# Odd-layer attention by heads: transposed scores, masked bias tables made in the projection, output projection and router as a stage of their own

## The chip, the cores and the metric

The kernel runs on one NeuronCore of a Trainium2 chip, as one launch. The metric is the device time of one execution in microseconds (us). Times below are for the whole program of two layers; the change touches one part of the second layer. The engines are TensorE (PE in the profile, with its weight loads as PEld), VectorE (DVE), ScalarE (ACT), GpSimd (POOL) and SyncE (SP); DMAs are issued by SP, ACT and POOL.

## The reference, cut to what matters

Two layers over 1024 latent tokens (a grid of 16 rows of 64 columns) and 256 context tokens, model width 1024, float32. The second (odd) layer projects to q, k and v of 8 heads of width 64 and to a convolution branch. q and k are normalised per head. Each latent query sees 8 grid rows by 16 grid columns around it, with a bias per head and relative position, and all 256 context tokens:

```python
def row_block(args):
    qr, ridx, ri = args
    kr = jnp.take(kg, ridx, axis=1)[:, :, col_idx]
    vr = jnp.take(vg, ridx, axis=1)[:, :, col_idx]
    bias = jnp.transpose(rpb_cols[:, ridx - ri + NA_MAX_ROWS - 1], (0, 2, 1, 3))
    s_loc = jnp.einsum('bchd,bicjhd->bhcij', qr, kr, ...) * scale + bias
    s_ctx = jnp.einsum('bchd,bshd->bhcs', qr, k_ctx, ...) * scale
    p = jax.nn.softmax(jnp.concatenate([s_loc..., s_ctx], axis=-1), axis=-1)
    ...
```

The heads' outputs and the convolution's (512 columns each) go through the output projection (1024 x 1024), a gate and the residual; then come a second norm and a router with 16 logits, and the mixture of experts. In the odd layer only latent tokens are needed behind the attention.

## The kernel before, in words

Tokens lie in tiles of 128: 8 latent (LT) and 2 context (CT) ones. Stages follow each other with a barrier of all engines between them; in a stage every engine has its own program and waits on semaphores. Matrix products whose exactness matters are split: an operand is rounded to a high part (`hi`, type fp32r) and a rest (`lo`), and three products hi*hi, hi*lo, lo*hi are summed in PSUM.

`project_odd` (tiles `po_...`, L941) loops over 10 token tiles. `NormStage` loads, normalises, transposes and modulates a tile: ACT rounds it (L339), POOL makes the rest (`rest_lo`, L343) and the inverse root (`root`, L305), DVE scales the next tile (L310). PE makes q, k and v (72 matmuls of 512 columns). For the per-head norms ACT squares, DVE sums (L1057), POOL raises to -1/2 (L1029), DVE multiplies (L1067, L1068). PE transposes k (L1086), ACT and DVE split it into `kT1_hi` and `kT1_lo` (L1007, L1074), which stay in SBUF with `v1`. q goes to DRAM (`q_d`). SP writes each row of the bias table 64 times to DRAM (`rpb_d`, L981), so that a read with a skewed stride gives a table over query and key columns.

`attend(nc, k, 1, ...)` (tiles `at_...`, L1199) walks over `AttendPlan.events`, an order written out for all engines: for each of 8 query tiles 8 heads. One (tile, head) is a unit: PE makes scores with the 128 queries on partitions (three products, L1597) over 4 or 5 key tiles and 2 context tiles, DVE adds the table and takes the maximum (L1474, L1478, L1482), ACT takes the exponential with the row sum (L1356), PE transposes the probabilities tile by tile (L1610), ACT and DVE copy them (L1369, L1493), and PE multiplies each 128 x 128 piece with 64 columns of v (L1575). Tables come by DMA for each head and each of three groups of tiles (`load_table`, L1336), and POOL adds the masks (L1409, L1413). Between the units of a tile lie the steps of the tile before: `heads`, `mixed`, two halves of the output projection (L1563), the residual on POOL (L1435), the norm, and the router (also L1563, 24 matmuls of 16 columns).

`attend_even` (L1730) is layer 0's attention. It is not changed, and its lines L1858, L1981, L2070, L2071 and L2078 work on transposed scores: keys on partitions, 512 columns of queries.

## Time and profile before

| | |
|---|---|
| median of 3 runs | 3467.13 us (3462.18 to 3471.53) |
| the profiled execution, its own time | 3476.95 us |
| its span | 3475.2 us |
| projection of the odd layer, 2052.4 to 2306.4 us | 254.0 us |
| attention, output projection, router of the odd layer, 2306.4 to 2904.6 us | 598.2 us |
| busy over the span: PE, DVE, ACT, POOL | 79%, 44%, 29%, 15% |

The stages' borders are the first DMA that SP issues in each. Busy shares are averages over stages with different limits. [...]

### The profile page before, as it was taken

The numbers are of one execution on the slowest core, as the hardware profiler recorded it, in microseconds if no ns is written. First come the engines' busy times: TensorE is split into PE (matmuls) and PEld (weight loads), VectorE is DVE, ScalarE is ACT, GpSimd is POOL, SyncE is SP. The second block draws the span as 40 slices with busy tenths as digits, with TensorE's granted clock in tenths as the row PEclk, the third lists the DMA queues.
The fourth block names the chain that finished last, engine by engine and source line by source line (L and its number), as shares of the span: only waits on it lengthen the run. The fifth ranks groups of instructions, "written<-read, shape, count | busy, mean of one in ns | idle before, by whom it ended". The sixth has DMA issues, their size and how long they took to land. (4 is left out here: it accounts for less than half of the span.)

```text
span 3475.2 us, 34184 instructions
## 1 busy us (share of the span) xinstructions
PE 2733.7 (79%) x11887; PEld 2073.8 (60%) x11888; DVE 1535.6 (44%) x2403; ACT 1012.6 (29%) x1342; POOL 531.5 (15%) x485
## 2 busy tenths in 40 slices
PE   5499788897844999997068957868899992899991
PEld 0488455565611888885055325757788882688781
DVE  2255543334222566464623723333333332566754
ACT  1122232332302455452111112222222220455640
POOL 0233112011120000000230002320300112100001
PEclk9999798897956999998588978975666675899995
DMA  9110353110167777663700022242111113658855
GB/s 376 54 42 34 104 181 141 32 55 28 43 204 288 257 261 261 249 223 122 266 25 6 12 57 71 68 97 69 39 43 40 40 40 138 243 215 329 307 218 211
DMA packets 244213, 476.78 MB, mean 137 GB/s; under 512 B 85773, under 2 KB 99067, under 8 KB 237948
## 3 DMA queue, kind: packets, MB, share of 16 engines
q1 hardware_dynamic: 172312, 354.27, 29.4%
q0 software_dynamic: 19632, 65.66, 5.2%
q10 hardware_dynamic: 52148, 55.28, 4.8%
q8 instruction: 72, 1.18, 0.1%
q14 instruction: 49, 0.40, 0.0%
HBM read 387.70 MB, written 87.45 MB: 137 GB/s over the span
## 5 line engine op out<-in xcount | busy, mean ns | idle before, releaser
L2505 DVE TENSOR_TENSOR ex_gu_lo<-mw_gu,ex_gu_hi 128x2048 fp32r<-128x2048 f32 x128 | 287.4, 2288 | 78.0 <-ACT ex_gu_hi L2425 77.7
L2425 ACT ACTIVATE ex_gu_hi<-mw_gu 128x2048 fp32r<-128x2048 f32 x128 | 237.5, 1910 | 166.4 <-DVE ex_y L2552 160.6
L2078 PE MATMUL at_ps_o<-at_pT,at_v_one 128*128 128x512 f32 x336 | 186.3, 638 | 1.7 <-ACT at_pT L1858 1.7
L2583 PE MATMUL ex_ps_g<-ex_gu_hi,ex_xT_hi 128*128 128x512 f32 x408 | 169.7, 416 | 8.4 <-issue 5.2
L2583 PE MATMUL ex_ps_y<-ex_d_hi,ex_hT_hi 128*128 128x512 f32 x408 | 166.7, 409 | 9.1 <-DVE ex_d_lo L2505 7.7
L1858 ACT ACTIVATE at_pT<-at_ps_s 128x512 f32<-128x512 f32 x168 | 99.5, 595 | 233.5 <-PE at_ps_s L2071 233.2
L2505 DVE TENSOR_TENSOR ex_d_lo<-mw_d,ex_d_hi 128x2048 fp32r<-128x2048 f32 x64 | 143.8, 2289 | 53.4 <-ACT ex_d_hi L2425 53.4
L2583 PE MATMUL ex_ps_g<-ex_gu_lo,ex_xT_hi 128*128 128x512 f32 x408 | 164.4, 403 | 0.0
L2583 PE MATMUL ex_ps_g<-ex_gu_hi,ex_xT_lo 128*128 128x512 f32 x408 | 164.2, 402 | 0.0
L2583 PE MATMUL ex_ps_y<-ex_d_lo,ex_hT_hi 128*128 128x512 f32 x408 | 161.9, 397 | 0.0
L2583 PE MATMUL ex_ps_y<-ex_d_hi,ex_hT_lo 128*128 128x512 f32 x408 | 161.9, 397 | 0.0
L2583 PE MATMUL ex_ps_u<-ex_gu_hi,ex_xT_hi 128*128 128x512 f32 x408 | 161.2, 395 | 0.0
L2583 PE MATMUL ex_ps_u<-ex_gu_lo,ex_xT_hi 128*128 128x512 f32 x408 | 161.2, 395 | 0.0
L2583 PE MATMUL ex_ps_u<-ex_gu_hi,ex_xT_lo 128*128 128x512 f32 x408 | 161.1, 395 | 0.0
L1356 ACT ACTIVATE at_s<-at_s,at_nmx 128x768 f32<-128x768 f32 (+1 forms) x64 | 63.3, 989 | 318.4 <-DVE at_nmx L1482 318.4
L1575 PEld LDWEIGHTS at_ps_o<-v,at_pT 128*128 128x128 f32 x832 | 154.5, 283 | 1.4 <-issue 1.4
L2051 PE MATMUL at_ps_t<-k_both,at_q_both 128*128 128x512 f32 (+1 forms) x208 | 112.5, 581 | 54.5 <-DVE at_mx L1968 37.9
L1575 PE MATMUL at_ps_o<-v,at_pT 128*128 128x64 f32 x832 | 154.9, 363 | 0.5 <-ACT at_pT L1369 0.2
L2400 POOL TENSOR_TENSOR ex_at<-ex_slots,ex_nil 128x1 int32<-128x1 int32 x53 | 16.6, 312 | 804.1 <-PE ex_ps_x L2577 799.1
L1968 DVE TENSOR_REDUCE at_mx<-at_ps_t 128x1 f32<-128x512 f32 (+1 forms) x208 | 115.9, 583 | 48.0 <-PE at_ps_t L2051 46.6
L320 PE MATMUL pc_pt<-ident,pc_x 128*128 128x128 f32 x64 | 14.9, 409 | 148.2 <-DVE pc_x L310 148.2
L2425 ACT ACTIVATE ex_d_hi<-mw_d 128x2048 fp32r<-128x2048 f32 x64 | 119.1, 1909 | 28.3 <-DVE ex_y L2527 19.7
(456 smaller groups left out, 6400.2 us busy)
## 6 DMA issues: line engine op xcount, KB each, us to landing
mw_gu<-in_moe_w_gate SPq DMA_DIRECT2D x32, 2048.0 KB, 10.4
mw_gu<-in_moe_w_up SPq DMA_DIRECT2D x32, 2048.0 KB, 15.4
mw_d<-in_moe_w_down SPq DMA_DIRECT2D x32, 2048.0 KB
y_d<-ex_y ACTq DMA_DIRECT2D x51, 512.0 KB
mod_mod_w<-in_ada_w SPq DMA_DIRECT2D x24, 1024.0 KB, 11.0
ro_mod_w<-in_ada_w SPq DMA_DIRECT2D x24, 1024.0 KB, 19.8
y_d<-at_zero POOLq DMA_DIRECT2D x36, 512.0 KB, 5.2
x_d<-at_x SPq DMA_DIRECT2D x18, 512.0 KB, 2.6
```

The costliest lines, as they stand in the source:

```text
L320: mm = self.nc.tensor.transpose(self.pt[h][:, q, :], self.x[i % 2][:, c * P:(c + 1) * P], self.k.ident[:, :])
L1356: nc.scalar.activation(s[u % 3][:, 0:n], s[u % 3][:, 0:n], ACT.Exp, bias=nmx[:, u % 3:u % 3 + 1], accum_out=sums[:, i % 2, h:h + 1]).then_ ...
L1575: mm = nc.tensor.matmul(ps_o[i % 2][:, h * HD:(h + 1) * HD], pT[u % 2][:, c, :], values(kt, h), start=(c == 0), stop=(c == len(kts) - 1), ...
L1858: nc.scalar.activation(pT[u % 3][:, :], ps_s[u % 3][:, :], ACT.Exp).then_inc(S["exp_done"], 1)
L1968: nc.vector.tensor_reduce(mx[:, hd, c:c + 1], ps[:, :, :].rearrange("p c t -> p (c t)")[:, 0:runs[c][1]], AX.X, ALU.max).then_inc(read, 1)
L2051: nc.tensor.matmul(ps[:, :, :].rearrange("p c t -> p (c t)")[:, 0:n], q_both[i % 2][g][:, j * P:(j + 1) * P], k.k0_both[:, g, a:a + n], st ...
L2078: nc.tensor.matmul(ps_o[g][:, :], v_one[:, kt, g:g + 2, :].rearrange("p a d -> p (a d)"), pT[u % 3][:, :], start=(u == plan.first[i, g]), ...
L2400: nc.gpsimd.tensor_tensor(at[:, :], slots[:, bass.ds(within(n, most), 1)], nil[:, :], ALU.add).then_inc(S["at_ready"], 1)
L2425: nc.scalar.activation(dst, src, ACT.Copy).then_inc(sem, 1)
L2505: sub = lambda dst, a, b, sem: nc.vector.tensor_tensor(dst, a, as_f32(b), ALU.subtract).then_inc(sem, 1)
L2583: mm = nc.tensor.matmul(out, a[:, c, :], b[:, c, cols], start=(c == 0 and j == 0), stop=(c == chunks - 1 and j == 2))
```

## The change

The projection no longer keeps k and v in SBUF. It also transposes q, splits it, and POOL stores q, k (high and rest, transposed) and v to DRAM by its own DMA queue. POOL also makes the bias tables with the column mask in them: in 16 parts it loads a part of a mask table (`skews`, 480 KB broadcast), adds the bias rows, and stores 480 KB to `rows_d`. There are two tables, for queries and for keys on partitions.

The attention works on units (head, half of the queries): 16 units of 8 steps, each step one key tile against up to 512 queries. First come maxima: for each query tile one product with rounded operands, whose maximum over keys becomes a shift; it is transposed and put as a 65th row into the query operand. Then per step: two products for the scores, DVE adds the table, ACT takes the exponential, one product with v beside a block of ones gives outputs and sums. All operands of a head come by 19 DMAs; two heads' buffers exist. The output projection and the router run as a new stage behind it, over 8 tiles.

```diff
-def project_odd(nc, k, w_in, q_norm, k_norm, rpb):
+def project_odd(nc, k, w_in, q_norm, k_norm, rpbs, skews):
...
+        PART = 8
...
+                        nc.scalar.activation(v[j % 2][:, :], ps_v[:, :], ACT.Copy).then_inc(S["v_copied"], 1)
                         act.wait_ge(S["kT_full"], i)
+                        nc.scalar.activation(k_hi[j % 2][:, :, :], ps_kT[:, :].rearrange("p (c t) -> p c t", c=4), ACT.Copy
+                                             ).then_inc(S["kT_hi"], 1)
                         if j < LT:
-                            act.wait_ge(S["q_ready"], i)
-                            act.dma_start(k.q_d[j * P:(j + 1) * P, :], qk[:, 0:BW]).then_inc(S["q_out"], 16)
+                            act.wait_ge(S["qT_full"], i)
+                            nc.scalar.activation(q_hi[j % 2][:, :, :], ps_qT[:, :].rearrange("p (c t) -> p c t", c=4), ACT.Copy,
+                                                 scale=HD ** -0.5).then_inc(S["qT_hi"], 1)
...
+                def store_heads(j):
+                    p, t = j % 2, slice(j * P, (j + 1) * P)
+                    pool.wait_ge(S["kT_done"], j + 1)
+                    parts = [(k.kh_d, k_hi), (k.kl_d, k_lo)]
+                    if j < LT:
+                        pool.wait_ge(S["qT_done"], j + 1)
+                        parts += [(k.qh_d, q_hi), (k.ql_d, q_lo)]
+                    for dst, src in parts:
+                        pool.dma_start(dst[:, t].rearrange("(c p) t -> p c t", p=P), as_f32(src[p][:, :, :])).then_inc(head_out[p], 16)
+                    pool.wait_ge(S["v_copied"], j + 1)
+                    pool.dma_start(k.v_d[t, :], v[p][:, :]).then_inc(head_out[p], 16)
+                def load_skew(n):
+                    o, part = divmod(n, GRID_W // PART)
+                    pool.dma_start(skew[n % 2][:, :, :].rearrange("p c x -> p (c x)"),
+                                   skews[o, part * PART * P:(part + 1) * PART * P].partition_broadcast(8 * 15)).then_inc(S["skew_in"], 16)
+                def mask_rows(n):
+                    o, part = divmod(n, GRID_W // PART)
+                    pool.wait_ge(S["rows_in"], 32)
+                    pool.wait_ge(S["skew_in"], 16 * (n + 1))
+                    if n >= 2:
+                        pool.wait_ge(S["rows_out"], 16 * (n - 1))
+                    nc.gpsimd.tensor_tensor(rows[n % 2][:, :, :], skew[n % 2][:, :, :], bc(bias_rows[o][:, :], 1, PART), ALU.add
+                                            ).then_inc(S["rows_made"], 1)
+                    pool.wait_ge(S["rows_made"], n + 1)
+                    pool.dma_start(k.rows_d[o].rearrange("h r c x -> (h r) c x")[:, part * PART:(part + 1) * PART, :], rows[n % 2][:, :, :]
+                                   ).then_inc(S["rows_out"], 16)
+                    if n + 1 < 2 * GRID_W // PART:
+                        load_skew(n + 1)
...
+                        if j:
+                            store_heads(j - 1)
+                            for n in (2 * j - 2, 2 * j - 1):
+                                if n < 2 * GRID_W // PART:
+                                    mask_rows(n)
+                store_heads(NT - 1)
...
+                        if j < LT:
+                            dve.wait_ge(S["qT_hi"], i)
+                            nc.vector.scalar_tensor_tensor(q_lo[j % 2][:, :, :], ps_qT[:, :].rearrange("p (c t) -> p c t", c=4), HD ** -0.5,
+                                                           as_f32(q_hi[j % 2][:, :, :]), ALU.mult, ALU.subtract).then_inc(S["qT_done"], 1)
...
+                    if j < LT:
+                        pe.wait_ge(S["q_ready"], j + 1)
+                        if j:
+                            pe.wait_ge(S["qT_done"], j)
+                        for c in range(4):
+                            mm = nc.tensor.transpose(ps_qT[:, c * P:(c + 1) * P], qk[:, c * P:(c + 1) * P], k.ident[:, :])
+                        mm.then_inc(S["qT_full"], 1)
...
-def key_plan(l, tile):
...
-class AttendPlan:
...
-def attend(nc, k, l, w_out, colmask, rowmask):
...
+class OddPlan:
+    def __init__(self):
+        self.units = [(h, g) for h in range(8) for g in range(2)]
+        self.steps, self.first, self.last = [], {}, {}
+        for u, (h, g) in enumerate(self.units):
+            self.first[u] = len(self.steps)
+            local = self.local(g)
+            self.steps += [(u, LT, 0, 4)] + local[:3] + [(u, LT + 1, 0, 4)] + local[3:]
+            self.steps[self.first[u]:] = [(u, *s[1:]) for s in self.steps[self.first[u]:]]
+            self.last[u] = len(self.steps) - 1
...
+        nu = len(self.units)
+        for u in range(nu):
+            for s in range(self.first[u], self.last[u] + 1):
+                at = s - self.first[u]
+                if u + 1 < nu and at < 4:
+                    self.event('max', u + 1, at)
+                if at == 2 and u and self.units[u - 1][0] % 2:
+                    self.event('normal', u - 1)
+                if u + 1 < nu and at == 6:
+                    self.event('shift', u + 1)
+                if s % 4 == 3 and s // 4 < 16:
+                    self.event('weights', s // 4)
+                if s + 2 < len(self.steps):
+                    self.event('scores', s + 2)
+                self.event('values', s)
+            self.event('drain', u)
+        self.event('normal', nu - 1)
+    def local(self, g):
+        return [(0, kt, max(kt - 2, 0) if kt > 3 else 0, min(kt + 3, 4)) if g == 0 else
+                (0, kt, 0 if kt < 7 else 1, min(kt - 1, 2) if kt < 4 else 4) for kt in range(2 * g, 2 * g + 6)]
...
+def attend_odd(nc, k, w):
...
+                def rows(dst, o, h, r0, n):
+                    ap = bass.AP(k.rows_d.tensor, ((o * 8 + h) * 15 + r0) * GRID_W * P + P // 2 - 1,
+                                 [[P - 1, GRID_W], [GRID_W * P, n], [1, GRID_W]])
+                    sp.dma_start(dst.rearrange("p (s c) -> p s c", s=n), ap).then_inc(head_in[h % 2], 16)
+                for h in range(8):
+                    p = h % 2
+                    if h >= 2:
+                        sp.wait_ge(S["valued"], plan.last[2 * (h - 2) + 1] + 1)
+                    r = slice(h * HD, (h + 1) * HD)
+                    for dst, src in ((qb[p][0:HD, :], k.qh_d), (qb[p][HD:P, :], k.qh_d), (kb[p][0:HD, :], k.kh_d), (kb[p][HD:P, :], k.kl_d)):
+                        sp.dma_start(as_f32(dst), src[r, :]).then_inc(head_in[p], 16)
+                    for half in range(2):
+                        s = slice(half * GRID_W, (half + 1) * GRID_W)
+                        rows(inner[p][s, half * GRID_W:(half + 8) * GRID_W], 0, h, 3, 8)
+                        for g, r0 in enumerate((5, 1)):
+                            rows(edge[p][s, g, :], 0, h, r0 - half, 10)
+                    sp.dma_start(as_f32(qr[p][0:HD, :]), k.ql_d[r, :]).then_inc(head_in[p], 16)
+                    sp.dma_start(as_f32(k1[p][0:HD, :]), k.kh_d[r, :]).then_inc(head_in[p], 16)
+                    for half in range(2):
+                        s = slice(half * GRID_W, (half + 1) * GRID_W)
+                        rows(innerT[p][s, (half + 1) * GRID_W:(half + 9) * GRID_W], 1, h, 4, 8)
+                        for g, r0 in enumerate((1, 5)):
+                            rows(edgeT[p][s, g, :], 1, h, r0 - half, 10)
...
+                    if what == 'scores':
+                        s, (u, kt, c0, c1) = i, steps[i]
+                        n = (c1 - c0) * P
+                        if s >= 3:
+                            act.wait_ge(S["valued"], s - 2)
+                        if kt < LT:
+                            act.wait_ge(S["added"], plan.added[s])
+                            src = sb[(plan.added[s] - 1) % 2]
+                        else:
+                            act.wait_ge(S["scored"], s + 1)
+                            src = ps_s[s % 2]
+                        nc.scalar.activation(pT[s % 3][:, 0:n], src[:, 0:n], ACT.Exp).then_inc(S["exp_done"], 1)
...
+                        if (j < 2) == (g == 0):
+                            slot = (2, 0)[j % 2] * GRID_W
+                            nc.vector.tensor_tensor_reduce(junk[j % 2][:, 0:512], ps[:, 0:512], edge[p][:, g, slot:slot + 512], 1.0, -3.0e38, ALU.add,
+                                                           ALU.max, mx[g][:, j, 0:1])
+                            nc.vector.tensor_reduce(mx[g][:, j, 1:2], ps[:, 512:512 + CT * P], AX.X, ALU.max).then_inc(read, 1)
+                        else:
+                            nc.vector.tensor_tensor_reduce(junk[j % 2][:, :], ps[:, 0:10 * GRID_W + CT * P], inner[p][:, :], 1.0, -3.0e38, ALU.add,
+                                                           ALU.max, mx[g][:, j, 0:1]).then_inc(read, 1)
...
+                        dve.wait_ge(S["scored"], s + 1)
+                        nc.vector.tensor_tensor(sb[(m - 1) % 2][:, 0:n], ps_s[s % 2][:, 0:n], tab[:, slot * GRID_W:slot * GRID_W + n], ALU.add
+                                                ).then_inc(S["added"], 1)
+                    elif what == 'normal':
+                        h, g = units[i]
+                        dve.wait_ge(S["drained"], i + 1)
+                        nc.vector.reciprocal(sums[:, g, :], sums[:, g, :]).then_inc(S["inverted"], 1)
...
+                        if s == plan.first[u]:
+                            emptied(pe, 'shift', u)
+                        if s >= 2:
+                            if steps[s - 2][1] < LT:
+                                pe.wait_ge(S["added"], plan.added[s - 2])
+                            else:
+                                pe.wait_ge(S["exp_done"], s - 1)
+                        keys, q = slice(kt * P, (kt + 1) * P), slice(g * 512 + c0 * P, g * 512 + c1 * P)
+                        nc.tensor.matmul(ps_s[s % 2][:, 0:n], kb[p][:, keys], qb[p][:, q], start=True, stop=False)
+                        nc.tensor.matmul(ps_s[s % 2][:, 0:n], k1[p][0:HD + 1, keys], qr[p][0:HD + 1, q], start=False, stop=True
+                                         ).then_inc(S["scored"], 1)
+                    elif what == 'values':
+                        s, (u, kt, c0, c1) = i, steps[i]
+                        h, g = units[u]
+                        n = (c1 - c0) * P
+                        pe.wait_ge(S["exp_done"], s + 1)
+                        if s == plan.first[u] and u >= 2:
+                            pe.wait_ge(S["drained"], u - 1)
+                        nc.tensor.matmul(ps_o[g][:, c0 * P:c1 * P], vo[h % 2][:, kt, :, :].rearrange("p a d -> p (a d)"), pT[s % 3][:, 0:n],
+                                         start=(s == plan.first[u]), stop=(s == plan.last[u])).then_inc(S["valued"], 1)
...
+def output_odd(nc, k, w):
...
+                for i in tiles:
...
+                        mm.then_inc(S["g_full"], 1)
+                        if i and not half:
+                            route(i - 1)
+                    if i:
+                        scores(i - 1)
+                route(LT - 1)
+                scores(LT - 1)
...
```

## Rows read from the trace of the kernel before

**Rows 1.** Windows: projection, attention to router, one query tile, layer 0's attention

```profile
core 0: us, PE busy (x) PEld busy (x) DVE busy (x) ACT busy (x) POOL busy (x), PEclk, DMA share, GB/s
2052.40:2306.40 254.00, 191.99 (x792) 151.00 (x792) 87.77 (x176) 55.72 (x84) 70.12 (x39) 0.88 0.26 70
2306.40:2904.60 598.20, 517.21 (x2528) 463.00 (x2528) 193.18 (x626) 140.25 (x266) 90.06 (x64) 0.66 0.19 53
2599.00:2667.00 68.00, 65.13 (x328) 58.83 (x328) 23.30 (x76) 16.63 (x32) 5.24 (x4) 0.70 0.11 37
380.00:1000.00 620.00, 512.40 (x1884) 341.58 (x1884) 241.72 (x406) 191.25 (x330) 88.96 (x92) 0.86 0.27 90
```

**Rows 2.** Groups by line and shape, same query tile, 2599 to 2667

```profile
L1575 PE MATMUL at_ps_o<-v,at_pT 128*128 128x64 f32 x112 | 20.6, 360 | 0.0
...
L1610 PE MATMUL at_ps_t<-ident,at_s 128*128 128x128 f32 x56 | 13.3, 373 | 0.0
...
L1563 PE MATMUL at_ps_g<-at_w_hi,at_aT_hi 128*128 128x512 f32 x16 | 7.2, 449 | 0.0
```

**Rows 3.** GpSimd's timeline, one tile of the projection

```profile
2186.10 2.91 POOL L1029 TENSOR_TENSOR po_r<-po_stat,mhalf 128x16 f32<-128x16 f32 x1 [2.20 <-DVE po_stat L1059]
2190.41 1.79 POOL L1033 TENSOR_TENSOR po_qk<-po_qk,po_gains 128x512 f32<-128x512 f32 x1 [1.40 <-DVE po_qk L1068]
2203.19 2.40 POOL L343 TENSOR_TENSOR po_lo<-po_hf,po_hi 128x1024 fp32r<-128x1024 f32 x1 [10.99 <-ACT po_hi L339]
...
2208.30 2.91 POOL L1029 TENSOR_TENSOR po_r<-po_stat,mhalf 128x16 f32<-128x16 f32 x1 [2.20 <-DVE po_stat L1059]
```

**Rows 4.** Timeline of all engines, the same tile

```profile
2197.50 0.60 PE L1086 MATMUL po_ps_kT<-ident,po_qk 128*128 128x128 f32 x4
...
2198.77 0.69 DVE L1074 TENSOR_TENSOR kT_lo<-po_ps_kT,kT_hi 128x512 fp32r<-128x512 f32 x1 [7.71 <-ACT kT_hi L1007]
...
2199.38 2.64 DVE L331 TENSOR_SCALAR po_hf<-po_pt,po_cols 128x128 f32<-128x128 f32 x8
```

**Rows 5.** DMAs issued by GpSimd: duration of the issue, time to landing

```profile
L1910 POOL DMA_DIRECT2D y_d<-at_zero x36: 533/533/672, 381.8 to 553.8; - x36
...
DMA to landing us min/median/max: 3.0/5.2/13.1
```

**Rows 6.** Timeline of layer 0, full clock, a float32 product and the next instruction

```profile
647.58 1.02 PE L2078 MATMUL at_ps_o<-at_pT,at_v_one 128*128 128x512 f32 x2
...
648.04 0.80 PE L2031 MATMUL at_ps_g<-at_w_hi,at_aT_hi 128*128 128x512 f32 x1
```

**Rows 7.** Timeline, half clock, two products of 512 columns in a row

```profile
1785.08 0.63 PE L352 MATMUL pc_ps_g<-cw_w_lo,pc_hi 128*128 128x512 f32 x1
...
1785.51 0.63 PE L352 MATMUL pc_ps_g<-cw_w_hi,pc_lo 128*128 128x512 f32 x1
```

**Rows 8.** VectorE's groups by shape, attention of the odd layer

```profile
L1474 DVE CUSTOM_DVE_ANT_0 at_s<-at_ps_s,at_table 128x320 f32<-128x320 f32 x64 | 29.6, 489 | 31.0 <-POOL at_table L1413 15.5 <-PE at_ps_s L1597 13.2 <-issue 1.1
L1478 DVE TENSOR_SCALAR_CACHE_REDUCE at_s<-at_ps_s 128x256 f32<-128x256 f32 x64 | 27.0, 422 | 3.8 <-PE at_ps_s L1597 2.5
...
L1529 DVE TENSOR_TENSOR at_tmp<-at_ps_g,at_gate 128x512 f32<-128x512 f32 x16 | 11.1, 692 | 115.8 <-PE at_ps_g L1563 115.8
```

**Rows 9.** VectorE's reciprocal in layer 0's attention

```profile
L1981 DVE RECIPROCAL at_sums<-at_sums 128x512 f32<-128x512 f32 x10 | 33.4, 3337 | 9.3 <-ACT at_total L1868 9.3
```

**Rows 10.** ScalarE's exponential in layer 0's attention

```profile
L1858 ACT ACTIVATE at_pT<-at_ps_s x168: 577/597/612, 409.5 to 938.7; 128x512 f32<-128x512 f32 x168
```

**Rows 11.** DMA queues, 2324 to 2330: only 256-byte packets of tables

```profile
q10 hardware_dynamic: 4701, 1.17, 129.9%
```

**Rows 12.** DMA issues, 2242 to 2272: KB, us to landing

```profile
rpb_d<-po_bias_rows SPq DMA_DIRECT2D x1, 3840.0 KB, 27.7
```

**Rows 13.** Window 2312 to 2315, start of the attention: last number GB/s

```profile
2312.00:2315.00 3.00, 0.00 (x0) 0.00 (x0) 0.00 (x0) 0.00 (x0) 0.00 (x0) 0.50 1.04 363
```

**Rows 14.** Window of one router product, line L1563 alone

```profile
2604.79:2608.47 3.68, 3.68 (x24) 3.68 (x24) 0.72 0.41 131
```

944 lines of the change are left out of this document (407 added, 537 removed).

## Prediction, made before the changed kernel was run

> **What bounds the kernel now.** I read the windows by stage first. The change touches two stages of the span of 3475.2 us: the odd layer's projection, 254.0 us, and attention with output projection and router, 598.2 us [rows 1]. In the second PE is busy 517 of 598 us, and in a steady query tile 65.1 of 68.0 us; DVE has 23 and ACT 17 of those 68. So PE sets the end, at a mean clock of only 0.70 in that tile (layer 0's attention: 0.86) [rows 1]. The groups of that tile show where PE's time goes: 20.6 us for 112 products with only 64 columns, 13.3 us for 56 transposes of probabilities, while the output projection's 48 products of 512 columns take about 3 x 7 us [rows 2]. Head by head, PE spends its time on instructions that stream few columns.
>
> The projection is bound by a loop through several engines, not by PE: GpSimd's power (L1029) starts at 2186.10 and again at 2208.30, a period of 22.2 us [rows 3]. Between them GpSimd ends L1033 at 2192.20 and idles 11.0 us until `rest_lo` (L343). That waits for PE's transposes, DVE's modulation and ACT's rounding [rows 3, 4]; behind it on GpSimd stand `root` and the next power, and for these wait DVE's scaling and the next tile's products.
>
> **Projection.** It adds four transposes of q (0.4 us, by those of k) and DVE's q rest (0.69 us as L1074), both ahead of the modulation L331 [rows 4]: +1.1 us a tile if nothing else is later. ACT's copies (0.6 us) and the dropped q store move nothing.
>
> GpSimd's new work, put into the 11.0 us: five stores a tile. One issue takes 0.53 us with 128 pieces [rows 5]; four of the new ones have 512 pieces, which no row shows. I take 1.0 us for each (bounds 0.53 and four times that, 2.1), in all 4.6 us with v's 0.6. A mask add on 120 x 1024 elements costs 2.4 us as L343 [rows 3], with a store and a load issued behind it 3.6 us; two a tile. The second add waits for the mask part whose load was issued just before: landing took 3.0 to 13.1, median 5.2 us for 512 KB [rows 5]; I take 5.0. Sum: 4.6 + 3.6 + 5.0 + 3.6 = 17 us, 6 more than are free. Then GpSimd is the loop: 28 us for the eight tiles that make tables (8 x 6 = 48), 2 us for the rest, 4 us for the last stores: 254 + 54 = **308 us**. Bounds: stores at 0.53 and landing in 3.0 give 13 us of work: 254 + 8 x 2 + 6 = 276. Stores at 2.1 and landing at 6 give 22: 254 + 88 + 6 = 348. The dropped `rpb_d` write (27.7 us [rows 12]) ended before the stage did; worth 0.
>
> **Attention, PE and DVE of a unit.** The removed work is the whole 598. Of a new unit PE streams 3328 columns once for maxima, 3328 twice for scores and 3328 for values in float32. A float32 product of 512 columns takes 0.46 us at full clock, 647.58 to 648.04, two passes of 0.23 [rows 6]; at 1.2 GHz one pass takes 0.43 [rows 7]. That is 32.5 passes: 7.5 us, or 14.0 at 1.2 GHz. DVE has more: from 256 and 320 columns (0.42 and 0.49 us) a slope of 1.05 ns per column [rows 8]. A maximum over 896 columns is 1.09 + 0.08, one over 512 and 256 is 0.69 + 0.08 + 0.42: four together 4.7 us. Six adds on 2304 columns are 3.3 us, minus-maximum 0.2. In half of the units comes a reciprocal of 3.34 us [rows 9], 1.7 on average, in the middle of the maxima. All maxima lie in the first four steps: there DVE needs 8.5 us and gaps, 9.3, and PE waits. The last four steps have PE: 2.6 us, about 1.2 us while ACT puts the shift row in place ahead of the next unit's first scores, and the chain product, add, exponential (0.60 us [rows 10]): 4.5. Sum 13.8 us at full clock; at half clock the first part is PE's 10 and the second 7: 17. I take U = **15 us**. ACT's 7 us a unit are hidden.
>
> **Attention, loads of a head.** 12 of the 19 loads are tables in pieces of 256 bytes, with v 2.16 MB. Alone, such pieces moved at 1.17 MB in 6 us, 195 GB/s [rows 11]: 11.1 us. The other 1.77 MB and 0.5 MB of output weights go at some 300 GB/s, between that and the 363 of large pieces [rows 13]: 7.6 us; with 2.3 us to land L = **21 us** (bounds: 17, all near 300 to 363; 33, all at the 3.93 MB in 27.7 us of the table write [rows 12], with landing). A head's loads are released when the head two before it is done, but the maxima of its first unit stand in the second unit of the head before: they have one unit of cover, 15 us, not two. PE and DVE both wait at the head of their queues, everything behind them too. Head period: 21 + 15 = 36 us instead of 30.
>
> Stage: 2 + 20 us for head 0 (all covers gone), 8 for four maxima, the exponential's table and a shift, 30 for head 0's units: 60. Six periods of 36: 216. The last head 30. Last reciprocal and splits 9, barriers 5. **320 us**. Bounds: U 13, L 17: 18 + 7 + 26 + 6 x 30 + 26 + 12 = 269. U 17, L 33: 33 + 9 + 34 + 6 x 50 + 34 + 15 = 425.
>
> [...]
>
> **Output stage.** Per tile 48 products: 11.2 us at 0.233; the router's 24 took 3.7 [rows 14]; eight transposes 0.9. The norm's chain runs beside the next tile's first half: DVE's product 0.69, GpSimd's adds, DVE's and GpSimd's passes over 1024 columns about 8 us, about PE's 3 + 5.6. At half clock a tile is 27. I take 17.5, as the small products let the clock fall: 140, with 10 to fill (gate rows, first split) and 15 for the last norm and router: **165 us** (148 to 200).
>
> **Sum.** 308 + 320 + 165 = 793 against 852.2: 59 us less. The profiled execution took 3476.95 us and becomes 3418; it lies 9.8 us over the median, so the median of 3467.13 becomes **3408 us**.
>
> **Rivals.**
> (a) The head loads are hidden after all, L under U: for it speaks that alternate halves of the partitions are filled; 36 us less: 3372. 15%.
> (b) GpSimd's additions fit in its idle 11 us (loads land in 3 us, stores cost 0.5): 6 a tile less, 1.1 stays: 3367. 12%.
> (c) The clock stays at 1.2 GHz through the attention: rows show 0.70 and 0.66 in the stage of before and 0.50 in its start, where PE is often idle [rows 1, 13]. U = 17 lengthens 16 units and not the loads: 20 us with fewer recoveries, with 10 in the output stage 3438. 12%. [...]
> (d) Slower: the head loads crawl. At 142 GB/s as the table write [rows 12] L is 33 and each of six periods 12 longer: 3480. It decides from L = 31. Against it: loads of the same pieces ran at 195 GB/s [rows 11]. 9%.
> (e) GpSimd's stores at 3 us each or more, issue by issue: 8 us x 8 more, 3472. 5%.
> (f) Both (a) and (b): 3331. 5%.
> The forecast itself: 42%, with its own range of 3375 to 3440.
>
> **Numbers.** 0.3% is about 10 us, what a measurement of this kernel tells from no change. Slower: (d), part of (e) and of the forecast's upper tail: 12%. Same: 7%. Faster: 81%. The range takes in (a), (b), (c), and (e): 3330 to 3475.
>
> **What would show it.** Right: in the projection GpSimd's L1029 every 27 to 29 us and no idle time before `rest_lo`; in the attention PE and DVE waiting some 6 us, six times, for loads of a head, once in 36 us; DVE the fullest engine of a unit's first half, with reciprocals of 3.3 us. The forecast is wrong if GpSimd's period stays near 23 or goes beyond 34, if the head period is 30 or 48, or if the output stage's tiles take over 20 us.

## The result, and the profile after

The changed kernel takes 3489.05 us (median of 4 runs, 3487.29 to 3496.10) beside 3466.55 us for the kernel before (4 runs, 3462.18 to 3471.53): a ratio of 1.0058 with a 95% interval of 1.0041 to 1.0076. It is slower by 0.6%, where 1.7% faster was forecast, and it lies outside the range. The kernel before, run again beside later experiments, had medians of 3465 to 3473 us; beside the highest of these the slowdown would be 16 us and not 22. The profiled execution took 3487.29 us, with a span of 3485.5.

I read the stages first. The windows go from the first transfer of one stage on the SP queue to that of the next: projection, attention, output stage. PEclk is the TensorE clock that was granted, as a share of full speed; its mean over the span is 0.84 in the kernel before and 0.86 in this one.

```profile
core 0: us, PE busy (x) PEld busy (x) DVE busy (x) ACT busy (x) POOL busy (x), PEclk, DMA share, GB/s
2051.30:2380.80 329.50, 208.74 (x824) 164.00 (x824) 92.63 (x184) 59.19 (x92) 158.49 (x134) 0.80 0.43 120
2380.80:2743.20 362.40, 218.46 (x736) 139.28 (x736) 148.11 (x299) 109.42 (x201) 50.52 (x50) 0.77 0.62 99
2743.20:2915.00 171.80, 145.34 (x640) 121.35 (x640) 34.32 (x58) 23.12 (x41) 53.79 (x40) 0.81 0.28 99
```

Beside [rows 1]: the projection has grown from 254.0 to 329.5 us, and the 598.2 us of attention, output projection and router are now 362.4 + 171.8 = 534.2. That is 75.5 us lost and 64.0 won. What stands behind took 570.6 us and takes 570.5; of the 11.5 us the span shows 10.3, as the projection began 1.1 earlier. In the attention PE's busy time fell far, and is only 218 of 362 us, with DVE at 148: no engine is full there. The DMA share has risen from 0.19 to 0.62. The question is what everyone waits for.

**Projection.** GpSimd's timeline of one tile, to set beside [rows 3]; in brackets the idle time ahead and what ended it.

```profile
2142.64 2.91 POOL L1073 TENSOR_TENSOR po_r<-po_stat,mhalf 128x16 f32<-128x16 f32 x1 [2.21 <-DVE po_stat L1112]
2146.95 1.79 POOL L1077 TENSOR_TENSOR po_qk<-po_qk,po_gains 128x512 f32<-128x512 f32 x1 [1.40 <-DVE po_qk L1121]
2148.68 0.88 POOL L1033 DMA_DIRECT2D kh_d<-po_k_hi  x1
2149.57 0.76 POOL L1033 DMA_DIRECT2D kl_d<-po_k_lo  x1
...
2152.38 2.40 POOL L1049 TENSOR_TENSOR po_rows<-po_skew,po_bias_rows 120x1024 f32<-120x1024 f32 x1
...
2155.61 0.54 POOL L1039 DMA_DIRECT2D po_skew<-in_k_skew  x1
2163.96 2.40 POOL L1049 TENSOR_TENSOR po_rows<-po_skew,po_bias_rows 120x1024 f32<-120x1024 f32 x1 [7.81 <-DMA po_skew<-in_k_skew]
...
2167.73 2.35 POOL L343 TENSOR_TENSOR po_lo<-po_hf,po_hi 128x1024 fp32r<-128x1024 f32 x1
2170.03 0.56 POOL L305 TENSOR_TENSOR po_rstd<-po_ms,mhalf 128x1 f32<-128x1 f32 x1
2172.79 2.91 POOL L1073 TENSOR_TENSOR po_r<-po_stat,mhalf 128x16 f32<-128x16 f32 x1 [2.20 <-DVE po_stat L1112]
```

The power comes 30.15 us later, and ahead of L343 there is no idle time left where [rows 3] had 10.99. So GpSimd is the loop, as forecast. The one hole is the 7.81 us ahead of the second mask addition, which waits for the load that L1039 has just issued; it was forecast at 5.0. The five stores cost 3.7 us, not 4.6.

This isn't so in all eight tiles that make tables. In the first five the wait is 7.8 to 8.4 us and the period 30.1 to 30.7; in the last three the wait is 5.5 to 5.6, and the one full period among them is 27.95. The first line is SP's, the second GpSimd's in the sixth of these tiles:

```profile
2156.19 0.32 SPq L275 DMA_DIRECT2D po_x<-x_d  x1
...
2313.42 2.40 POOL L1049 TENSOR_TENSOR po_rows<-po_skew,po_bias_rows 120x1024 f32<-120x1024 f32 x1 [5.58 <-issue]
```

In each of the five tiles with the long wait SP issues the load of a later token tile (L275, 512 KB) 0.6 to 1.9 us after GpSimd has issued the mask part's; in the other three there is no such load left. The five stores stand ahead of the mask load in all eight. So in this trace the long wait goes with the second load beside it, and without it the landing was close to the 5.0 us forecast.

**Attention.** The queue's issues on SP show when a head's loads are released, and PE's timeline when its first maximum begins.

```profile
2443.95 1.11 SPq L1753 DMA_DIRECT2D at_qb<-qh_d  x2
...
2492.80 1.11 SPq L1753 DMA_DIRECT2D at_qb<-qh_d  x2
```

```profile
2471.05 0.80 PE L1924 MATMUL at_ps_t<-at_kb,at_qb 128*128 128x512 f32 x1 [15.03 <-DMA at_edgeT<-rows_d]
2522.50 0.79 PE L1924 MATMUL at_ps_t<-at_kb,at_qb 128*128 128x512 f32 x1 [11.09 <-DMA at_edgeT<-rows_d]
```

From the release at 2443.95 to the first maximum at 2471.05 are 27.1 us, for the next head 2492.80 to 2522.50, 29.7. These are the two longest of six: the others take 26.0, 23.9, 24.1 and 23.4, and the mean is 25.7. From the first maximum to the next release are 21.75 and, to 2536.91, 14.41 us, and so on in turn, with a mean of 18.7 over five. The releases of heads 2 and 7 stand at 2443.95 and 2668.05: a mean period of 44.8 us, forecast at 36. Windows in one such load, the last three with all engines still:

```profile
2446.00:2449.00 3.00, 3.00 (x12) 2.00 (x12) 2.84 (x7) 1.64 (x3) 0.00 (x0) 1.00 1.16 203
2449.00:2452.00 3.00, 2.89 (x12) 1.60 (x10) 2.16 (x6) 1.14 (x3) 1.82 (x2) 1.00 1.06 249
...
2461.00:2464.00 3.00, 0.00 (x0) 0.00 (x0) 0.00 (x0) 0.00 (x0) 0.00 (x0) 0.50 1.03 208
2464.00:2467.00 3.00, 0.00 (x0) 0.00 (x0) 0.00 (x0) 0.00 (x0) 0.00 (x0) 0.50 1.37 156
2467.00:2470.00 3.00, 0.00 (x0) 0.00 (x0) 0.00 (x0) 0.00 (x0) 0.00 (x0) 0.50 1.23 139
```

What moves in a window is told by its packets. In the first, more than half of the bytes are v's, in pieces of 256 bytes on ScalarE's queue; in the third more than a third are output weights. The second holds q, k and output weights in pieces of some 3 to 5 KB and next to nothing else: 249 GB/s, and two such windows in the next head's load show 186 and 171. The last two hold table pieces of 256 bytes alone: 156 and 139, and 159 in the next head. I had taken 300 and 195.

A second wait was not foreseen. This is the timeline of DVE, GpSimd, ScalarE and PE around a reciprocal:

```profile
2477.45 3.35 DVE L1901 RECIPROCAL at_sums<-at_sums 128x512 f32<-128x512 f32 x1
...
2480.89 1.26 POOL L1836 TENSOR_TENSOR at_a<-at_total,at_sums 128x512 f32<-128x512 f32 x1 [22.34 <-DVE at_sums L1901]
...
2482.18 0.63 ACT L1806 ACTIVATE ow_a_hi<-at_a 128x512 fp32r<-128x512 f32 x1 [4.95 <-POOL at_a L1836]
2482.84 0.60 ACT L1784 ACTIVATE at_pT<-at_ps_s 128x512 f32<-128x512 f32 x1
...
2483.49 0.79 PE L1949 MATMUL at_ps_s<-at_qb,at_kb 128*128 128x512 f32 x1 [4.41 <-ACT at_pT L1784]
```

ScalarE's rounding L1806 waits for GpSimd's product, that for DVE's reciprocal, and the exponentials are queued behind the rounding: PE idles 4.41 us. Over the stage PE waits so seven times, 29.5 us in all; three of the seven lie in a unit that covers a load. Behind the wait PE starts at a granted clock of 0.50 and keeps it up to 2489 (0.69 on the mean from 2483.49 to 2492.80).

**Output stage.** Windows in one tile:

```profile
2780.00:2782.00 2.00, 2.00 (x11) 2.00 (x11) 0.00 (x0) 0.00 (x0) 0.00 (x0) 0.50 0.20 76
2782.00:2784.00 2.00, 2.00 (x6) 1.71 (x7) 0.88 (x3) 0.00 (x0) 0.56 (x1) 0.50 0.00 0
2784.00:2786.00 2.00, 2.00 (x6) 1.52 (x6) 0.64 (x1) 0.00 (x0) 1.28 (x1) 0.50 0.00 0
...
2788.00:2790.00 2.00, 2.00 (x13) 1.64 (x12) 0.14 (x1) 0.00 (x0) 0.00 (x0) 1.00 0.96 295
```

In a tile PE waits 2.07 us for DVE ahead of the router's products of 16 columns; within these the granted clock falls to 0.50 and stays there through some nine of the wide products: they start 0.43 us apart, and 0.23 at 1.00. From tile to tile it takes 20.0 us in five cases of six, not 17.5.

### The profile page after: what moved, and what is told of

It reads as the page before. It is cut to its first block and busy times, and to the rows that moved or that the text cites. A ratio compares the mean times of both kernels' runs of the same rounds, so it can differ in the third digit from the quotient of the medians.

```text
span 3485.5 us, 31738 instructions
## 1 busy us (share of the span) xinstructions
PE 2594.6 (74%) x10767; PEld 1883.2 (54%) x10768; DVE 1530.2 (44%) x2142; ACT 1007.7 (29%) x1326; POOL 632.4 (18%) x606
## 5 line engine op out<-in xcount | busy, mean ns | idle before, releaser
L1959 PE MATMUL at_ps_o<-at_pT,at_vo 128*128 128x512 f32 (+3 forms) x256 | 129.8, 593 | 1.4 <-ACT at_pT L1784 1.4
L926 PE MATMUL pc_ps_c<-pc_yT,pc_diag 128*128 128x512 f32 x248 | 107.3, 593 | 1.6 <-ACT pc_acc L766 1.6
L1567 PEld LDWEIGHTS at_ps_t<-k_both,at_q_both 128*128 128x128 f32 x208 | 43.9, 211 | 118.3 <-DVE at_mx L1484 73.0
```

The lines of the kernel that those rows point to most:

```text
L926: mm = nc.tensor.matmul(ps_c[:, :], diag[c][:, t, :], yT[:, c, q * QT + t:q * QT + t + QT], start=(t == 0), stop=(t == CONV - 1))
L1567: nc.tensor.matmul(ps[:, :, :].rearrange("p c t -> p (c t)")[:, 0:n], q_both[i % 2][g][:, j * P:(j + 1) * P], k.k0_both[:, g, a:a + n], st ...
L1959: nc.tensor.matmul(ps_o[g][:, c0 * P:c1 * P], vo[h % 2][:, kt, :, :].rearrange("p a d -> p (a d)"), pT[s % 3][:, 0:n], start=(s == plan.fi ...
```

## The experiments

Ratios are against the kernel before; the changed kernel's is 1.0058. A saving in us against the changed kernel is the difference of the two ratios times 3467, good to some 8 us; where less matters, I go by the length of the stage in the profiled execution, measured as above.

### e1_ahead: the mask parts loaded two ahead

```diff
-                    if n + 1 < 2 * GRID_W // PART:
-                        load_skew(n + 1)
+                    if n + 2 < 2 * GRID_W // PART:
+                        load_skew(n + 2)
...
                 load_skew(0)
+                load_skew(1)
```

with one semaphore for each of the two buffers, for loads and for stores.

> Projection only: the load of mask part n+2 is issued after the add of part n, so every load has a tile's time to land; nothing is left out. Theory (the second add of a tile waits 7.8 to 8.4 us for a load issued right before it, and this wait is on the loop that sets the tile's period): GpSimd's power comes every 22.5 to 24 us instead of 30.1 to 30.7, the projection goes from 329.5 to about 277 us, and the kernel takes about 3437 us. Rival 1 (the 7.8 us are transfers queued behind the tile's own stores, so the load lands as late however early it is issued): period 28 to 30, 3475 us. Rival 2 (store issues and adds themselves fill the loop): period 26 to 27, 3460 us.

Measured: 3439.43 us, ratio 0.9912 (0.9886 to 0.9937), 51 us saved. The projection took 278.8 us. GpSimd's timeline:

```profile
2184.24 2.40 POOL L1051 TENSOR_TENSOR po_rows<-po_skew,po_bias_rows 120x1024 f32<-120x1024 f32 x1
...
2188.03 2.41 POOL L1051 TENSOR_TENSOR po_rows<-po_skew,po_bias_rows 120x1024 f32<-120x1024 f32 x1
...
2192.41 2.40 POOL L343 TENSOR_TENSOR po_lo<-po_hf,po_hi 128x1024 fp32r<-128x1024 f32 x1 [0.62 <-ACT po_hi L339]
```

No idle time is left between the additions, and GpSimd is 0.62 us early at L343: from the power at 2174.53 to the next at 2197.53 are 23.0 us. The wait for the mask part was on the loop with its full length; both rivals fall. The rest of GpSimd's new work, some 11 us a tile, fits almost exactly into what was idle before; the stage is still 25 us longer than it was, half of it from the last tile of latent tokens on.

### e2_mask_first: both mask parts ahead of the five stores

```diff
                         if j:
-                            store_heads(j - 1)
                             for n in (2 * j - 2, 2 * j - 1):
                                 if n < 2 * GRID_W // PART:
                                     mask_rows(n)
+                            store_heads(j - 1)
```

> Projection only, nothing left out: GpSimd makes both mask parts of a tile before it issues the tile's five stores. Theory (a mask part lands in 7.8 us and not in 5 because it is queued behind 1.3 MB of the tile's stores): the wait ahead of the second add falls to 4.5 to 5.5 us, the period from 30.4 to about 27.5, kernel 20 to 25 us below the changed kernel, about 3468 us. Rival (the 7.8 us are the load's own: 120 partitions filled from one row): the wait stays at 7 to 8.5, period 30 or more, kernel within 5 us of the changed one, about 3490 us.

Measured: 3483.32 us, ratio 1.0020 (1.0005 to 1.0034), 13 us saved; by the stage 6 us (323.1 us). The wait is 6.66 us in the first tile and 5.6 to 5.9 in the other seven, the periods are 29.0 and then 28.0 to 28.6. So the result lies between the two expectations, but it doesn't show that the stores were what the load waited for. The new order also moved the mask load away from the load of a token tile, which is now issued 4 us or more behind it (2.6 in the first tile); and in the changed kernel, where no token tile is loaded beside it, the wait is 5.5 us with all five stores ahead. Both runs fit a load of 5.5 to 6 us of its own and 2 to 3 more for the 512 KB beside it. No run moves that load alone.

### e3_no_tables: no tables for heads 2 to 7

```diff
-                    for half in range(2):
+                    for half in range(2 if h < 2 else 0):
                         s = slice(half * GRID_W, (half + 1) * GRID_W)
...
```

and the same for the transposed tables, with the counts of the waits to match.

> Leaves out the 12 table loads of heads 2 to 7 (these heads use the tables of heads 0 and 1). Theory (the load of a head, 27 to 30 us against a cover of one unit, sets the head period): a head's remaining 2.1 MB land in 8 to 12 us, inside a unit; PE has no wait for a load at a head's first maximum, the head period goes from 44 to 49 us to 32 to 36, attention from 362 to 295 us, kernel about 3420 us. Rival 1 (the units themselves have grown, by the wait behind the reciprocal and a clock of 1.2 GHz, and would fill the period anyway): period 40 or more, kernel 3460 us or more.

Measured: 3422.17 us, ratio 0.9859 (0.9834 to 0.9884), 69 us saved; attention 292.7 us, head period 32.4. At heads 2 to 7 PE waits for a load three times, 2.2, 1.6 and 0.3 us, where it waited six times and 61.9 us in all. The load of a head set the period. The stages behind the router take their old time here, so the kernel's times can be compared. The waits at the reciprocals stayed, 4.8 us the longest, and the period is at 32 in spite of them.

### e4_long_pieces and e9_whole: what makes the load long

In e4_long_pieces a table load becomes

```diff
-                    sp.dma_start(dst.rearrange("p (s c) -> p s c", s=n), ap)
+                    sp.dma_start(dst, k.kh_d[h * HD:(h + 1) * HD, 0:n * GRID_W])
```

> Loads other data (rows of the stored keys) of the same bytes, into the same half of the partitions, in pieces of 2048 and 2560 bytes instead of 256, in place of the tables. Theory (the pieces of 256 bytes make the load of a head long): load 15 to 19 us instead of 27 to 30, head period 36 to 38, kernel about 3435 us. Rival 1 (the bytes, or the 64 partitions that each transfer fills, are what takes the time): load 25 us or more, head period 43 or more, kernel 3475 us or more.

In e9_whole each pair of transfers into 64 partitions becomes one into 128:

```diff
-                    for dst, src in ((qb[p][0:HD, :], k.qh_d), (qb[p][HD:P, :], k.qh_d), (kb[p][0:HD, :], k.kh_d), (kb[p][HD:P, :], k.kl_d)):
-                        sp.dma_start(as_f32(dst), src[r, :]).then_inc(head_in[p], 16)
+                    for dst, src in ((qb[p][:, :], k.qh_d), (kb[p][:, :], k.kh_d)):
+                        sp.dma_start(as_f32(dst), src[0:P, :]).then_inc(head_in[p], 16)
...
+                    rows(inner[p][:, GRID_W:8 * GRID_W], 7)
+                    for g in range(2):
+                        rows(edge[p][:, g, :], 10)
```

> Loads other data in place of q, k and the tables, as in e4_long_pieces in pieces of 1792 to 5120 bytes, but each transfer into all 128 partitions (9 transfers on the SP queue instead of 18, each twice as large; per head 3% fewer bytes). Theory (a transfer that fills 64 partitions moves at 220 to 250 GB/s, and this is why long pieces saved only 4 us of the load): 300 to 360 GB/s, from a head's release to its first maximum 16 to 18 us instead of 22.8, head period 36 to 38, kernel about 3445 us. Rival (it is the bytes, at what this path reads and writes, whatever the partitions): 220 to 250 GB/s, 21 to 23 us, kernel within 8 us of e4_long_pieces, about 3480 us.

Both change the attention's values, and with them what the router chooses: behind the router these two take 584.7 and 584.3 us instead of 570.5. Their own times (e4_long_pieces 3480.94 us, ratio 1.0029, 1.0014 to 1.0044; e9_whole 3447.90 us, ratio 0.9939, 0.9917 to 0.9960) hold 14 us that don't belong to the question, so I read the attention: 339.9 and 298.6 us, against 362.4. First e4_long_pieces, the head released at 2443.18, PE's first maximum and two windows:

```profile
2465.95 0.79 PE L1922 MATMUL at_ps_t<-at_kb,at_qb 128*128 128x512 f32 x1 [10.68 <-DMA at_edgeT<-kh_d]
```

```profile
2458.00:2461.00 3.00, 0.00 (x0) 0.00 (x0) 0.00 (x0) 0.00 (x0) 0.00 (x0) 0.50 1.04 222
2461.00:2464.00 3.00, 0.00 (x0) 0.00 (x0) 0.00 (x0) 0.00 (x0) 0.00 (x0) 0.50 1.07 227
```

and e9_whole, the head released at 2443.97:

```profile
2461.79 0.79 PE L1918 MATMUL at_ps_t<-at_kb,at_qb 128*128 128x512 f32 x1 [5.74 <-DMA at_edgeT<-kh_d]
```

```profile
2446.00:2449.00 3.00, 3.00 (x13) 2.02 (x12) 2.87 (x7) 1.61 (x3) 0.00 (x0) 1.00 1.06 362
2449.00:2452.00 3.00, 2.92 (x12) 1.60 (x10) 2.16 (x6) 1.14 (x3) 1.82 (x2) 1.00 1.02 342
2452.00:2455.00 3.00, 2.13 (x8) 1.29 (x9) 0.29 (x1) 1.34 (x4) 0.00 (x0) 1.00 1.06 277
2455.00:2458.00 3.00, 1.05 (x7) 0.79 (x5) 0.29 (x1) 2.50 (x5) 1.25 (x1) 1.00 1.04 225
```

The load of head 2 goes from 27.1 to 22.8 us with long pieces (4.3 less, and 22 us of attention), and to 17.8 with whole transfers (5.0 less again, with 3% fewer bytes). In e4_long_pieces the full windows of the load show 222 to 258 GB/s and its mean is 209; the period is 41.3 us, above what the theory on pieces allowed. In e9_whole the mean over the load is 263, from 362 in its first full window down to 225, and the period is 35.5. So of the 9.3 us between the changed kernel's load and e9_whole's, pieces of 256 bytes are less than half; v keeps its short pieces in both. The larger part goes with transfers into 64 partitions. What in such a transfer is slow, e9_whole doesn't separate: it also has about half as many transfers, twice as large, and two of its ten on the SP queue, those of `qr` and `k1`, still fill 64 partitions (its expectation speaks of nine, all whole).

### e5_early_tables: the maxima's tables released a unit earlier

```diff
                     if h >= 2:
+                        sp.wait_ge(S["nmx_done"], 2 * (h - 2) + 2)
+                    for half in range(2):
...
+                        rows(inner[p][s, half * GRID_W:(half + 8) * GRID_W], 0, h, 3, 8, max_in)
+                        for g, r0 in enumerate((5, 1)):
+                            rows(edge[p][s, g, :], 0, h, r0 - half, 10, max_in)
+                    if h >= 2:
                         sp.wait_ge(S["valued"], plan.last[2 * (h - 2) + 1] + 1)
```

The maxima wait for `max_in` (these six and the four of q and k), the first scores of the head for `head_in` (the other nine).

> Nothing is left out: the six tables for the maxima of head h are loaded as soon as the last maxima of head h-2 are done, a unit earlier than before; q and k follow at the old release and have a semaphore with these tables, the other nine loads have one of their own and are waited for at the first scores, a unit later. Theory (what is late is the release, not the rate): the wait of 14 us at a head's first maximum falls to under 2, nothing takes its place, head period 32 to 36, kernel about 3420 us. Rival 1 (the rate: 4 MB a head at 150 to 180 GB/s take 25 us of the period however early they start, and the wait moves to the first scores): head period 38 to 42, kernel 3455 us.

Measured: 3403.98 us, ratio 0.9815 (0.9790 to 0.9840), 84 us saved; attention 278.4 us, head period 31.3. Of these 84 us 68 lie in the five periods, 9 ahead of head 2's release and 7 behind head 7's. In PE's timeline from 2438 to 2502, over two heads, the waits of 2 us and more are these:

```profile
2460.92 0.80 PE L1958 MATMUL at_ps_s<-at_qb,at_kb 128*128 128x512 f32 x1 [4.78 <-ACT at_pT L1790]
2481.18 0.58 PE L1958 MATMUL at_ps_s<-at_qb,at_kb 128*128 128x256 f32 x1 [4.15 <-ACT at_pT L1790]
```

The bytes and their pieces are all still there, and from head 2 on no load is waited for: with this order of releases and waits the slow transfers cost nothing. Rival 1 falls. Two things were changed at once, the earlier release of six tables and the later wait for nine of the other loads; which carries how much, no run separates. The 9 us ahead of head 2 belong to the second, as the loads of the first heads wait for no release: PE's wait at head 0 is 28.0 us instead of 38.5. That, and q and k released late (waits of 2.2 and 1.6 us), is most of what e3_no_tables saved less.

### e6_split_later and e12_late: the wait behind the reciprocal

In e6_split_later ScalarE's rounding and GpSimd's rest get an event of their own:

```diff
+                if at == 5 and u and self.units[u - 1][0] % 2:
+                    self.event('split', u - 1)
                 self.event('values', s)
...
-                    elif what == 'normal':
+                    elif what == 'split':
                         h, g = units[i]
                         act.wait_ge(S["a_ready"], h // 2 * 2 + g + 1)
```

> Nothing is left out: ScalarE's rounding of a normalized unit and GpSimd's rest stand three steps later than the reciprocal and the product, so that ScalarE's exponentials are not queued behind them. Theory (ScalarE waits 5 us for the reciprocal and GpSimd's product, PE 4.4 us behind its exponential, six times of eight seen in the trace, and the clock drops with it; three of the eight lie in the unit that covers a load, where they cost nothing): ScalarE's wait for the product under 0.5 us, kernel 20 to 25 us below the changed kernel, about 3468 us. Rival 1 (DVE's reciprocal of 3.35 us itself holds up the adds behind it and PE waits as long): less than 8 us, 3482 us or more. Rival 2 (all eight count): 45 us, 3445 us.

In e12_late the reciprocal and the product are at step 5 as well, the rounding at step 7.

> The changed kernel with reciprocal, product and rounding at steps 5, 5 and 7 instead of 2, 2 and 2, and nothing else. Theory: both parts of the wait go, 25 to 30 us below the changed kernel, about 3462 us. Rival (half of these waits lie where a head's load sets the time, and the other half shows only in part): 10 to 18 us below it, 3475 us, no better than e6_split_later.

Measured: e6_split_later 3475.76 us, ratio 1.0004 (0.9991 to 1.0016), 19 us saved, by the attention stage 9 (353.4 us); e12_late 3474.49 us, ratio 1.0010 (0.9999 to 1.0020), 17 us saved, by the stage 15 (347.0). In e6_split_later's timeline ScalarE and PE still stand still behind the reciprocal:

```profile
2486.49 3.35 DVE L1907 RECIPROCAL at_sums<-at_sums 128x512 f32<-128x512 f32 x1
...
2491.87 0.69 PE L1955 MATMUL at_ps_s<-at_qb,at_kb 128*128 128x384 f32 x1 [2.51 <-DVE at_sb L1902]
2491.91 1.23 ACT L1787 ACTIVATE at_pT<-at_sb 128x512 f32<-128x512 f32 x2 [4.49 <-DVE at_sb L1902]
```

This lies between the theory and rival 1. ScalarE no longer waits for GpSimd, but for the additions queued on DVE behind the reciprocal, and PE's 4.4 us became 2.5. In e12_late the wait has moved again: PE waits up to 3.2 us for ScalarE's shift row, and the saving is the 10 to 18 us of its rival. The wait is real, and what these two orders take back is 9 to 19 us of the 71 by which the three stages miss. Neither order took away the most of PE's 29.5 us; whether another would, no run tells.

### e7_router_between: the router's products among the wide ones

```diff
+                            if i and half and c >= 4:
+                                scores(i - 1, 2 * (c - 4), 2 * (c - 3))
...
-                    if i:
-                        scores(i - 1)
```

and DVE makes the rest of the normalized row ahead of its product for the second half.

> Output stage only, nothing left out: the 24 products of the router of tile i-1, with 16 columns each, stand in eights' pairs between the products of 512 columns in the second half of tile i, and DVE makes the rest of the normalized row ahead of its product for that half. Theory (a tile takes 20 us and not 17.5 because PE waits 2.07 us for DVE ahead of the router and then falls to 1.2 GHz in the 24 small products and the nine after them): no wait there, granted clock 1.0 in a tile, 15.5 to 16.5 us a tile, stage 172 to about 143 us, kernel about 3462 us. Rival (the tile is bound by the chain of the norm through GpSimd, ScalarE and DVE): 18.5 to 19.5 us a tile, 3480 us or more.

Measured: 3472.43 us, ratio 0.9989 (0.9979 to 0.9999), 24 us saved; the stage took 152.1 us.

```profile
2790.00:2800.00 10.00, 8.95 (x56) 7.94 (x56) 1.57 (x3) 1.72 (x3) 3.52 (x3) 1.00 0.38 131
2800.00:2810.00 10.00, 8.23 (x42) 6.67 (x42) 3.71 (x7) 2.24 (x4) 4.19 (x3) 1.00 0.29 105
```

The clock stays at 1.00, and a tile takes 16.5 us (stores of x at 2801.80, 2818.33, 2834.85). The wait ahead of the router's products is gone, but PE now idles 1.8 us in each tile ahead of the transposes:

```profile
2807.57 1.09 PE L2117 MATMUL ou_ps_h<-ident,ou_h 128*128 128x128 f32 x8 [1.76 <-POOL ou_h L2064]
```

So of the 3.5 us that a tile became shorter, 0.3 are idle time and the rest goes with the clock. Order of products and idle time were changed together; which of them kept the clock up isn't separated. The stage has 9 us more than expected: the second tile took 19.2 us, and some 18 us up to the first store and 16 behind the last stand outside the tiles.

### e8_all, e10_no_split and e11_all_late: the edits together

e8_all joins e1_ahead, e5_early_tables, e6_split_later and e7_router_between; e10_no_split is that without the third; e11_all_late has e12_late's order in its place.

> Four edits in one, nothing left out: mask parts loaded two ahead (e1_ahead), the maxima's tables released a unit earlier (e5_early_tables), the rounding later (e6_split_later), the router's products between the others (e7_router_between). By their single gains (51 and 83 us measured, all eight waits of 5 us here since no load hides them, 30 us in the output stage): 3490 - 51 - 83 - 38 - 30 = about 3290 us. Rival (with the waits gone the loads of 4 MB a head at 190 GB/s are the bound of the head period, 27 us or more, and the late rounding gains nothing): 3325 us.

> e8_all without the later rounding, nothing left out. Theory (the gains of the four edits add up, 51 + 83 + 19 + 24 = 177 us of 3490, since e8_all measured 3318): 19 us above e8_all, about 3337 us. Rival (with the loads hidden all eight waits of 5 us lie open): 35 to 40 us above it, 3355 us.

> e8_all with the reciprocal on DVE and GpSimd's product three steps later too (at step 5 of 8, when the unit's maxima are done, and ScalarE's rounding at step 7); nothing is left out. Theory (of the wait behind the reciprocal, ScalarE's part went with the later rounding, but DVE's 3.35 us still stand between two adds in the middle of the maxima: ScalarE waits 4.5 us for the add, PE 2.8 us, eight times, and the clock falls behind it): PE's wait under 1 us, 15 to 20 us below e8_all, about 3300 us. Rival (at step 5 the chain product, add, exponential has as little slack, and the 3.35 us show there): within 5 us of e8_all, 3318 us.

Measured: e8_all 3318.27 us, ratio 0.9550 (0.9532 to 0.9568); e10_no_split 3333.32 us, ratio 0.9624 (0.9606 to 0.9641); e11_all_late 3313.53 us, ratio 0.9537 (0.9520 to 0.9554). The savings measured one by one (51 + 84 + 19 + 24 = 178) bring the changed kernel's 1.0058 to 0.9545, and e8_all has 0.9550: they add up, and my 3290 was 28 us too low, 19 of them because it counted all eight waits at the reciprocals at 5 us and 6 for the output stage. The stages of e8_all are 279.9, 259.2 and 151.6 us, and its head period is 29.0. In e10_no_split the attention takes 278.9 us and the period is 31.3, so the later rounding is worth 20 us here, as the theory had it; the rival's 35 to 40 fall. e11_all_late is 5 us below e8_all, the size of its rival, and not 15 to 20. Two heads of e8_all:

```profile
2391.52:2420.36 28.84, 24.39 (x93) 15.50 (x92) 17.79 (x36) 14.47 (x27) 9.80 (x11) 0.94 1.02 174
2420.36:2448.58 28.22, 24.41 (x93) 15.52 (x93) 17.70 (x36) 14.47 (x27) 9.80 (x11) 0.94 1.06 177
```

PE is now busy 24.4 of 28.5 us, and the DMA share is over 1 in the whole of both heads, at 174 and 177 GB/s. Yet the loads don't set this period: from 2391 on none of PE's waits ends with one. They end with DVE's add (15.5 us in six waits up to 2570) and ScalarE's shift row (8.1 us in twelve), and SP stands ready 6 us before the release at 2420.36. In e11_all_late the waits for the add are gone, those for the shift row have grown to 21.7 us, and the period is 28.0. How much shorter it could get before the loads are late again, no run tells.

## Why the prediction was wrong

The step that failed is the head period of the attention: a load of 21 us and one unit of 15 give 36, and the runs show 44.8, a load of 26.2 and 18.7 for the unit (five periods). The structure of that sum held; both of its terms were too small. The two other stages each have one such term, the landing of the mask part and the length of an output tile.

By the three stages the forecast was 793 us and 863.7 were measured, 70.7 more. Put on the forecast for the profiled execution, 3418, this gives 3489 against 3487.29, so nothing outside the three terms is missing. Between the medians the miss is 81 us; the other 10 come from taking off 9.8 us for the profiled execution of before, while that of after lies 1.8 under its median.

- **Projection, 308 us; 329.5.** The step held: GpSimd becomes the loop, with no idle time ahead of `rest_lo`. The mis-sized term is the landing wait inside its 17 us, 5.0 taken and 7.8 to 8.4 measured in five tiles, partly made up by stores of 3.7 instead of 4.6 us. Five periods of 30.35 instead of 28 are 12 of the 21.5 us. Another 2 come from the base: [rows 3] show a period of 22.2, but the mean of the six in the kernel before was 21.6. The other 7 or so lie in the last tiles and at the start. In three tiles the landing took 5.5 us, near the forecast; what I left out is the token tile's 512 KB that land at the same time in the other five. e1_ahead shows that this one wait is worth 51 of the 75.5 us that the stage grew.
- **Attention, 320 us; 362.4.** This is where the prediction fell. Of the parts, head 0 was 63.2 us against 60, five head periods 224.1 against 180, and from the last release to the end 75.1 against 80. The head period's structure, L + U with one unit of cover, was right: e3_no_tables and e5_early_tables took the wait away by two different ways. L was the larger mis-sized term: 23.4 to 29.7 us for 21, 5 of the 9 us that a period misses. Inside it, "the other 1.77 MB at some 300 GB/s" moved at 171 to 249 in the windows that hold little else, and the tables at 139 to 159 instead of 195. By e9_whole the first goes with transfers into halves of the partitions, which I had noted as a point for rival (a). The second doesn't: the loads of [rows 11] filled halves of the partitions too, in the same pieces, and why they ran at 195 GB/s stays open. The 2.3 us to land that are part of the forecast's 21 stand in no row, and no run shows them by themselves: the runs show L as a whole. U was 18.7 us and not 15, the other 4: 21.2 to 22.0 where a reciprocal's wait lies in it, 14.0 and 14.4 where none does. I had priced the reciprocal as 1.7 us of DVE time and never asked who is queued behind ScalarE's rounding.
- **Output stage, 165 us; 171.8.** Tiles of 20.0 us instead of 17.5. The clock was foreseen to fall at the small products, but not that it stays down for nine of the wide ones, and PE's 2.07 us behind DVE's order was missed. The start was cheaper than taken.
- **Rivals.** (a) and (b) fall: loads and waits lay open. (c) is true in part: the mean clock is 0.77 in attention and 0.81 in the output stage, and the windows in the waits show 0.50, but with the wait gone the clock comes back by itself (0.94 in e8_all), so it followed the waits. (d) was the nearest, at 9%: L did not reach its 31, nor did the rate fall to 142 over a load, yet the period of 44.8 us is nearly its 48, since U grew too. Rival (e) had the right place, with another price: issues of 0.75 us, and the landing in their stead. No single rival gave the result. Terms in all three stages missed to the same side, and the range didn't hold the case where they do. That the total of (d), 3480 us, comes so near is in part luck: it puts the whole miss on L.

## What to carry to other kernels

When a load is exposed, ask first when its buffer is released and which of its readers is last: an earlier release and a wait split in two brought 84 us with no byte less, and issuing a load two turns ahead brought 51. Price a transfer by rows of the same shape, in the number of partitions (a head's load of long pieces moved at 209 GB/s with most transfers into 64, at 263 with most into 128 and twice as large) as well as in the length of a piece, and with the load that will run beside it (the addition waited 7.8 to 8.4 us with 512 KB landing beside the mask part, 5.5 to 5.6 without). For every long instruction on an engine follow the whole chain to the first queue where something urgent stands behind it (a reciprocal of 3.35 us on DVE left PE idle for 4.41), and try small products between wide ones (the granted clock stayed at 1.00 in e7_router_between, where the idle time moved too).

## What the runs showed of the hardware

- With most transfers into 64 partitions and pieces of 2 to 5 KB a head's load moved at 209 GB/s on the mean, 222 to 258 in its full windows (e4_long_pieces); with most transfers into 128 partitions and twice as large at 263, 225 to 362 (e9_whole). The DMA engines' share in these windows was 1.02 to 1.22.
- Windows that hold pieces of 256 bytes alone showed 139 to 159 GB/s in the changed kernel (in the one of 139 the load ends, with under 115 GB/s in its last 0.6 us) and 195 in the kernel before, both into 64 partitions; the reason is open.
- A load of 480 KB issued by GpSimd kept the next addition waiting 7.8 to 8.4 us where 512 KB on the SP queue landed beside it, and 5.5 to 5.6 where nothing but GpSimd's own stores did.
- In the changed kernel the issue of a table load of 256-byte pieces on the SP queue took 0.60 us for a head's first table (2446.38), and 3.0 us for its fourth (2449.57), in the next head 4.8 (2498.40).
- Where the granted clock was 0.50, products of 512 columns started 0.43 us apart (changed kernel, 2782.83 to 2785.82), 1.2 columns a ns; this is the state that the forecast and the expectations call 1.2 GHz. Where it was 1.00 they started 0.23 us apart (2786.24 to 2789.43), 2.2 columns a ns.
- In a tile of the output stage PE idled 2.07 us and then ran 24 products of 16 columns without a gap, and the granted clock fell to 0.50 in the midst of these (after 10 of them at 2779.3, after 14 at 2799.8); with the wide products between them, and 1.8 us of idle time at another place of the tile, it stayed at 1.00 (e7_router_between).
- GpSimd's issue of a store with 512 pieces took 0.75 to 0.88 us, that of one with 128 took 0.56.
